# Projections begun inside the last head's step, and idle waits of TensorE filled with products that nobody reads

## The reference

```python
# first block: three branches of width 1024 each, one gated projection per branch
y_sb = stick_breaking_attention(sb_q, sb_k, sb_v)            # 8 heads of 128
y_s5 = s5_layer(s5_u, ..., s5_w_glu[l])                      # y * sigmoid(y @ w_glu)
y_ml = mlstm_chunkwise(ml_q_c, ml_k_c, ml_v, ...)            # 4 heads of 256
merged = jax.nn.sigmoid(g_sb) * (y_sb @ p_sb[l]) \
    + jax.nn.sigmoid(g_s5) * (y_s5 @ p_s5[l]) \
    + jax.nn.sigmoid(g_ml) * (y_ml @ p_ml[l])
x = x + gate1[:, None, :] * (merged @ w_out[l])
h = modulate(rms_norm(x, norm_moe_g[l]), shift2, scale2)
x = x + gate2[:, None, :] * hierarchical_moe(h, ...)         # 32 experts, top 2
x = rms_norm(x, final_g)
# second block: the same form with rglru (y_a), nsa (y_b, 8 heads), fox (y_c, 8 heads)
merged = (mg[:, :, 0] * (y_a @ w_branch[l, 0])
          + mg[:, :, 1] * (y_b @ w_branch[l, 1])
          + mg[:, :, 2] * (y_c @ w_branch[l, 2]))
h = h + merged @ w_out[l]
h = h + jax.nn.sigmoid(h @ w_ple_gate[l]) * e
```

## Time and profile before

| | |
|---|---|
| median of 3 runs | 3511.61 us (3509.37 to 3517.85) |
| the profiled execution | 3514.14 us, its span 3512.3 us |
| TensorE busy | 3034.3 us (86%) |
| POOL busy | 1687.8 us (48%) |
| DVE busy, ACT busy | 1183.7 us (34%), 1226.0 us (35%) |
| DMA, mean | 201 GB/s |

### The profile page before, as it was taken

The page is one execution under the profiler, slowest core; times in us unless marked ns, Lnnn a source line. Parts: engine busy times, 40 slices in busy tenths (PEclk is TensorE's granted clock), DMA queues, the critical chain, the costliest instruction groups (busy, mean ns, idle before and its releaser), DMA issues.

```text
span 3512.3 us, 52529 instructions
## 1 busy us (share of the span) xinstructions
PE 3034.3 (86%) x20592; PEld 2492.2 (71%) x20592; DVE 1183.7 (34%) x1660; ACT 1226.0 (35%) x1408; POOL 1687.8 (48%) x1296
## 2 busy tenths in 40 slices
PE   6999899898998987798889729778779988879898
PEld 1777588888898876443434229777779988869898
DVE  1488821134361323200000053265621124432335
ACT  1232332433544223211111124455534444444343
POOL 0000167676676764000000018745549976649897
PEclk8999989899999998899999959899989999989999
DMA  9432247375444865688899924432325543325443
GB/s 397 169 111 104 102 170 299 139 286 189 144 143 156 299 260 222 251 331 357 341 396 392 405 94 164 156 112 100 110 100 186 181 159 131 123 94 188 157 170 133
DMA packets 102014, 704.34 MB, mean 201 GB/s; under 512 B 11968, under 2 KB 15808, under 8 KB 17216
## 3 DMA queue, kind: packets, MB, share of 16 engines
q1 hardware_dynamic: 83088, 602.97, 45.9%
q10 hardware_dynamic: 15408, 74.86, 5.6%
q0 software_dynamic: 3392, 24.64, 1.7%
HBM read 723.92 MB, written 22.54 MB: 213 GB/s over the span
## 4 chain that ended last, share of the span: by engine, by line
PE 69%; DVE 11%; DMA 11%; ACT 6%; issue 3%; POOL 0%; DVEq 0%; ACTq 0%; SPq 0%; POOLq 0%
PE acc L549 58%; PE wk L549 10%; DMA ring<-in_moe 6%; DMA side_buf<-in_ada 2%; DMA stage<-in_ada 2%; ACT w_hi L1086 1%; ACT L1086 1%; DVE yl L1592 1%; DVE C_z L1595 1%; DVE rms_red L1604 1%; DVE C_sm L1592 0%; DVE A_t L1592 0%; DMA stage<-in_main 0%; ACT hb L1086 0%; ACT C_z L1086 0%
## 5 line engine op out<-in xcount | busy, mean ns | idle before, releaser
L525 POOL TENSOR_TENSOR w_lo<-stage,w_hi 128x512 fp32r<-128x512 f32 x1268 | 1672.8, 1351 | 1165.4 <-PE acc L549 720.4
L549 PE MATMUL acc<-xh,w_hi 128*128 128x256 f32 x3568 | 910.7, 294 | 29.0 <-DVE xl L1592 21.4
L549 PE MATMUL acc<-xl,w_hi 128*128 128x256 f32 x3568 | 897.8, 290 | 0.0
L549 PEld LDWEIGHTS acc<-xh,w_hi 128*128 128x128 f32 x3568 | 711.6, 199 | 72.6 <-issue 56.4
L549 PEld LDWEIGHTS acc<-xl,w_hi 128*128 128x128 f32 x3568 | 711.6, 199 | 0.7
L1086 ACT ACTIVATE w_hi<-stage 128x2048 fp32r<-128x2048 f32 x317 | 604.0, 1907 | 38.8 <-DMA stage<-in_main 38.7
L549 PE MATMUL acc<-xh,w_lo 128*128 128x256 f32 x3568 | 476.7, 287 | 0.4 <-POOL w_lo L525 0.4
L549 PEld LDWEIGHTS acc<-xh,w_lo 128*128 128x128 f32 x3568 | 451.9, 195 | 3.9 <-issue 2.3
L549 PE MATMUL acc<-ring,xg 128*64 128x512 f32 x1248 | 296.1, 616 | 55.0 <-DMA ring<-in_moe 54.3
L537 POOL DMA_DIRECT2D y_rows<-X_ysb x20 | 10.9, 547 | 638.0 <-ACT X_ysb L1086 638.0
L549 PEld LDWEIGHTS acc<-ring,xg 128*64 128x64 f32 x1248 | 96.9, 142 | 240.0 <-issue 239.1
(11 more groups left out here) (439 smaller groups left out, 3338.8 us busy)
## 6 DMA issues: line engine op xcount, KB each, us to landing
stage<-in_main SPq DMA_DIRECT2D x317, 1024.0 KB, 4.8
ring<-in_moe SPq DMA_DIRECT2D x234, 1024.0 KB
side_buf<-in_ada ACTq DMA_DIRECT2D x64, 1024.0 KB, 5.0
stage<-in_ada SPq DMA_DIRECT2D x32, 1024.0 KB, 8.1
stage<-in_sb SPq DMA_DIRECT2D x32, 1024.0 KB, 4.8
y_rows<-X_ysb POOLq DMA_DIRECT2D x19, 1024.0 KB, 10.2
x<-in_x ACTq DMA_DIRECT2D x1, 2048.0 KB, 12.7
out<-x SPq DMA_DIRECT2D x4, 512.0 KB, 5.4
```

What stands on the lines that cost most here:

```text
L525: last = pool.tensor_tensor(w_lo[:, k % 2, cs], stage[:, k, cs], w_hi[:, k, cs].bitcast(F32), ALU.subtract)
L549: return pe.matmul(o, w, r, start=start, stop=stop)
```

## The change

There are two parts.

**Opening and closing.** In the last step of each of the four head phases, where there was only the small work, `opening(name, i, tiles)` now does part of the output projection's chunks i = 0 to 3: for both output tiles all products with `w_hi` on the input tiles that are finished (7 of 8; in stage_b 6 of 8), and for i = 0 and 1 also those with `w_lo`. In the places where a step with a further head ran the small work in the middle of a chunk, it now runs between the two output tiles of the opening (`mid`). Behind the last step, `closing` adds what is left: the last tile (the last two in stage_b), and for i = 2 and 3 all 16 products with `w_lo`. Chunks 4 to 7 are as before. What is computed is the same.

**Spin products.** `spin(times, n)` multiplies `ones` by `ident`, 128x128 by 128 columns in plain float32, into columns of a PSUM bank that are free and that the next real product overwrites. It stands ahead of ten waits outside loops (glu 30, p_s5 24, wout 36, the channel sum and the router chunk behind wout 30 and 20, the combination of the experts 90, two channel sums 48 and 90, the first kv chunk 30, wout2 40 times) and, as `spin_in`, at the head of each step with a further head in stage_b (10, in 3 steps), stage_c (12, in 7 steps) and stage_d (5, in 7 steps).

```diff
+        def spin(times, n):
+
+            pe.wait_ge(evac_done, n - 3)
+            k = n % 4 if isinstance(n, int) else None
+            for _ in range(times):
+                mm(acc[:, k, T:T + P], ones[:], ident[:])
...
-        def beside(n, g, s, work):
+        def beside(n, g, s, work, name=None, i=0):
 
             if g is not None:
                 wide(*slot(n, g), mid=work if s is not None else None)
             else:
-                work()
+                opening(name, i, 7, mid=work)
...
+        def opening(name, i, tiles, h=yh, l=yl, mid=None):
+
+
+            k, q = slot(BASE[name] + i)
+            n = BASE[name] + i
+            pe.wait_ge(hi_ready, n + 1)
+            if n >= 4:
+                pe.wait_ge(evac_done, n - 3)
+            for c in range(2):
+                o = acc[:, k, c * T:(c + 1) * T]
+                for t in range(tiles):
+                    w = w_hi[:, k, (c * WT + t) * P:(c * WT + t + 1) * P]
+                    gm(o, w, h[:, t, :], c + t == 0)
+                    gm(o, w, l[:, t, :])
+                if mid and c == 0:
+                    mid()
+            if i < 2:
+                pe.wait_ge(lo_ready, n + 1)
+                for c in range(2):
+                    for t in range(tiles):
+                        gm(acc[:, k, c * T:(c + 1) * T], w_lo[:, k % 2, (c * WT + t) * P:(c * WT + t + 1) * P], h[:, t, :])
+
+        def closing(name, i, tiles, h=yh, l=yl):
+
+            k, q = slot(BASE[name] + i)
+            n = BASE[name] + i
+            for c in range(2):
+                for t in range(tiles, WT):
+                    w = w_hi[:, k, (c * WT + t) * P:(c * WT + t + 1) * P]
+                    gm(acc[:, k, c * T:(c + 1) * T], w, h[:, t, :])
+                    gm(acc[:, k, c * T:(c + 1) * T], w, l[:, t, :])
+            if i >= 2:
+                pe.wait_ge(lo_ready, n + 1)
+            for c in range(2):
+                for t in range(tiles if i < 2 else 0, WT):
+                    last = gm(acc[:, k, c * T:(c + 1) * T], w_lo[:, k % 2, (c * WT + t) * P:(c * WT + t + 1) * P], h[:, t, :],
+                              stop=t == WT - 1)
+            last.then_inc(chunk_done, 1)
...
             if g is not None:
                 plain(0, g)
+            else:
+                pe.wait_ge(yh_ready, 7)
+                opening("p_sb", 0, 7)
...
         pe.wait_ge(yh_ready, 8)
-        for t in range(8):
+        for i in range(4):
+            closing("p_sb", i, 7)
+        for t in range(4, 8):
             half(*slot(BASE["p_sb"] + t))
         pe.wait_ge(y5_ready, 9)
         beside_ada("g_sb", 0, wide)
+        spin(30, BASE["glu"])
         pe.wait_ge(y_split, 1)
         each(pe, BASE["glu"], 4, half)
         ada_columns(2, side_row[0])
+        spin(24, BASE["p_s5"])
         pe.wait_ge(y_split, 2)
...
             if s is not None:
+                if g is not None:
+                    spin_in(10, base_b, g, 2)
                 pe.wait_ge(qk_ready, s * 4 + 4)
...
                     wide(*slot(base_b + j, g, 2))
+                elif j < 4:
+                    opening("p_ml", j, 6)
...
+        spin(36, BASE["wout"])
         pe.wait_ge(mg_split, 1)
...
+        spin(30, BASE["router"])
         channel_sum(2)
+        spin(20, BASE["router"])
...
         pe.wait_ge(dg_ready, 1)
+        spin(90, BASE["kv"])
         pe.wait_ge(yg_in, 64)
...
+        spin(48, BASE["kv"])
         channel_sum(3)
+        spin(90, BASE["kv"])
         channel_sum(4)
+        spin(30, BASE["kv"])
...
+                    spin_in(12, base_c, g)
                 pe.wait_ge(c_d, s * NC_D + 1)
...
+                    spin_in(5, base_d, g)
                 pe.wait_ge(d_d, s * ND_D + 2)
...
+        spin(40, BASE["wout2"])
         pe.wait_ge(mg_split, 2)
```

More of the change, by code:

```diff
@@ L572, in chunk, with spin_in @@
             last.then_inc(chunk_done, 1)
+        def spin(times, n):
[3 more added lines that the diff above has]
+                mm(acc[:, k, T:T + P], ones[:], ident[:])
+        def spin_in(times, base, g, per=1):
+            k, q = slot(base, g, per)
+            pe.wait_ge(evac_done, q * 4 + k - 3)
+            for _ in range(times):
+                mm(acc[:, k, T:T + P], ones[:], ident[:])
         def wide(k, q, t=None, mid=None, split=None):
             chunk(k, q, 1, DT, xh, xl, mid, split)
-        def beside(n, g, s, work):
+        def beside(n, g, s, work, name=None, i=0):
             if g is not None:
@@ L599, in beside_plain, with gm @@
             else:
-                work()
+                opening("p_sb", j, 7, mid=work)
         def half(k, q, t=None):
             chunk(k, q, 2, WT, yh, yl)
+        def gm(o, w, r, start=False, stop=False):
+            return pe.matmul(o, w, r, start=start, stop=stop, skip_group_check=True)
+        def opening(name, i, tiles, h=yh, l=yl, mid=None):
[32 more added lines that the diff above has]
+            last.then_inc(chunk_done, 1)
         def half2(k, q, t=None):
@@ L709, in stage_a @@
                 plain(2, g)
+            else:
+                opening("p_sb", 2, 7)
             if s is not None:
@@ L778, in _ @@
             stage_b(i, i - 1)
+        pe.wait_ge(by_ready, 3)
         stage_b(None, 3)
         pe.wait_ge(by_ready, 4)
-        each(pe, BASE["p_ml"], 8, half)
+        for i in range(4):
+            closing("p_ml", i, 6)
+        each(pe, BASE["p_ml"] + 4, 4, half)
         beside_ada("g_ml", 2, wide)
+        spin(36, BASE["wout"])
         pe.wait_ge(mg_split, 1)
@@ L987, in stage_c @@
                 wide(*slot(base_c, g))
+            else:
+                opening("p_a", 0, 7)
             if s is not None:
@@ L995, in stage_c @@
                 last.then_inc(c_p, 1)
-            beside(base_c + 1, g, s, gates)
-            beside(base_c + 2, g, s, probs)
-            beside(base_c + 3, g, s, values)
+            beside(base_c + 1, g, s, gates, "p_a", 1)
+            beside(base_c + 2, g, s, probs, "p_a", 2)
+            beside(base_c + 3, g, s, values, "p_a", 3)
         stage_c(0, None, 0)
@@ L1006, in _ @@
         pe.wait_ge(c_d, 8 * NC_D)
-        each(pe, BASE["p_a"], 8, half)
+        for i in range(4):
+            closing("p_a", i, 7)
+        each(pe, BASE["p_a"] + 4, 4, half)
         each(pe, BASE["g_a"], 16, wide)
@@ L1049, in stage_d @@
                 wide(*slot(base_d, g))
-            beside(base_d + 1, g, s, scores)
-            beside(base_d + 2, g, s, probs)
-            beside(base_d + 3, g, s, values)
+            else:
+                opening("p_c", 0, 7)
+            beside(base_d + 1, g, s, scores, "p_c", 1)
+            beside(base_d + 2, g, s, probs, "p_c", 2)
+            beside(base_d + 3, g, s, values, "p_c", 3)
         heads(pe, stage_d)
         pe.wait_ge(d_d, 8 * ND_D)
-        each(pe, BASE["p_c"], 8, half)
+        for i in range(4):
+            closing("p_c", i, 7)
+        each(pe, BASE["p_c"] + 4, 4, half)
         each(pe, BASE["g_c"], 16, wide)
+        spin(40, BASE["wout2"])
         pe.wait_ge(mg_split, 2)
```

## The result

Predicted 3461 us (3438 to 3492). Measured in turn with the kernel before, on the same chip: 3460.5 us (median, 3457.9 to 3461.3) against 3513.1 (3509.4 to 3517.9). The ratio is 0.9848, 95% interval 0.9831 to 0.9865, so 53 us less by the medians. The profiled execution has a span of 3459.5 us.

What follows compares the result with a forecast made beforehand. It took TensorE's work, its waits and the lower clock behind them as the bound, POOL close behind. Openings 29 plus spin products 22 make 51 off 3511.6, giving 3461 us, range 3438 to 3492.

Steps and rivals of the forecast that it cites:

- Openings, stages a, c, d: Last steps and projections of these stages: projection products moved into TensorE's idle time gain 6.9, 13.1 and 9.2 us.
- Opening, stage_b: Stage_b's last step: the openings delay the `B_stm` products and DVE's last chain by 6.1 us, leaving a gain of 3.9.
- Stage_d: Spin products in stage_d's seven steps gain 1.1 us each, 8 in all, by keeping the clock up.
- Stage_b, loop: Spin products in three steps of stage_b gain 1.4 us each, 4 in all.
- Stage_c: Spin products in stage_c's seven steps gain 0.6 us each, 4 in all, with 3.1 us of the wait left idle.
- Groups outside loops: The ten spin groups outside loops gain 6 us together, 2.0 of it at p_s5 and 0 at the combination.
- Price of a constant product: Each spin product takes 0.225 us, 0.45 at the lower clock, and no group outlasts its wait while the clock stays up.
- The rule against the change: The skill says transposes against the identity do not count as clock activity, so products with `ident` might not hold the clock.
- The first rival: Spin products do not hold the clock and cost 50 us, the openings give 29 back: 3533 us; chance 0.04.
- The rests are too long: The clock falls in the idle time left behind each spin group, the spins give under 5: 3480 us; chance 0.22.
- eaten by the last steps: Openings delay DVE's and ACT's chains, giving 10 instead of 29: 3480 us, or 3496 with spins at 5; chance 0.12.
- everything closes: Openings give 33 and spin products 40: 3439 us; chance 0.12.

Runs made afterwards that it cites:

- run 1: The changed kernel with every `spin` and `spin_in` line left out, so openings and closings alone: 3484.9 us, ratio 0.9917 to the kernel before.
- run 2: Constant products alone, with the last steps and projections as in the kernel before: 3491.2 us, ratio 0.9941 to that kernel.
- run 4: The changed kernel with 14 constant products ahead of the wait for B_qk in stage_b's last step: 3455.9 us, ratio 0.9837 to the kernel before.
- run 3: The changed kernel with ten more constant products ahead of the wait for C_zc in seven steps of stage_c: 3454.6 us, ratio 0.9827 to the kernel before.
- run 8: The changed kernel with 22 constant products ahead of C_qs, 10 ahead of C_zc, 24 and 8 in the last steps of stage_c and stage_d: 3451.2 us.
- run 11: The changed kernel without the twelve constant products at the head of stage_c's steps: 3458.9 us, ratio 0.9842 to the kernel before.
- run 6: The changed kernel without the ten `spin` groups outside loops, the three `spin_in` kept: 3461.4 us, ratio 0.9855 to the kernel before.
- run 5: The changed kernel with each constant product written as two transposes of the same tiles: 3463.0 us, ratio 0.9858 to the kernel before.
- run 9: The changed kernel with 14 constant products in stage_b's last step, 20, 10, 24 in stage_c, 8 in stage_d's last step, 116 ahead of the combination: 3434.1 us.
- run 10: The changed kernel with 15 constant products instead of 5 at the head of stage_d's seven steps: 3478.9 us, ratio 0.9896 to the kernel before.
- run 7: The changed kernel with stage_a's opening of chunk 0 moved behind the last head's next small product: 3456.9 us, ratio 0.9845 to the kernel before.

## Why the prediction was right, step by step

- **The sum** was right (51 against 53), and so was its split: 29 and 22 predicted, 29 and 23 in runs 1 and 2. But the 22 was right by compensation, which is luck: by the marks the places give 5.9, 0.4, 13 and 7.5 where 4, 4, 8 and 6 stood. These 26.8 and the openings' 29.7 make 56.5; the two executions differ by 52.8. Most of the rest is 2.6 us lost in g_sb (1.1 of waiting for `side_buf` and a dip behind it, which run 1's trace doesn't have) and 1.1 from wout to the second block.
- **Openings, stages a, c, d**: 6.9, 13.1, 9.2 predicted, 6.3, 13.0, 9.4 found. The working held in its parts: between the marks POOL's first low part behind the last step came 2.7, 9.5 and 5.8 us earlier (3, 9 and 5 foreseen), the last-head products wait less than they are held up, and POOL's low parts then set the pace. POOL was the bound longer than foreseen: six low parts follow one another (29.9 us), not three, so the gain is counted at the seventh chunk. TensorE's waits in the closings of these three stages were 4.0 and 0.3 to 0.8 us, not 4 and 2.5: the clock fell in each first one, and the products behind it ran at half speed through what would have been the second. In stage_a the working on POOL and DVE held as well (the last section has the numbers).
- **Opening, stage_b**: 3.9 predicted, 1.0 found; this step failed, and it failed for a reason outside it. The opening alone gives 3.6 (run 1). In the changed kernel the products behind the 4.0 us wait for B_qk ran at 1.2 GHz for 10 us, with the first opening among them, and the B_stm products started 8.1 us behind DVE's instruction for their operand (1069.56 less 1061.50), where it was 0.75 before (1076.20 in the earlier trace rows less 1075.45): 7.3 late, 6.1 foreseen. Fourteen constant products gave 4.5 back (run 4). The prediction had counted constant products per loop step and never asked what the last step, which has none, would inherit: run 2 shows it without any opening, 1.8 us lost there.
- **Stage_d**: 8 predicted, 13 found (the first product of the last head comes 42.9 us earlier and the start of stage_d 29.8). The prediction valued one dip a step at 1.1 of 1.7 us, in seven steps. In the trace five of the seven had two dips of 3.4 us each, one behind the wait for E_qks and one behind that for E_z (1.9 us, filled by nothing), and the first and second had none. With the first wait filled both went, and such a step fell from 34.1 to 31.1. Only one of the seven kept one (32.6). So the number of steps was too high and the worth of one too low.
- **Stage_b, loop**: 4 predicted, 5.9 found.
- **Stage_c**: 4 predicted, 0.4 found; this step failed. It said that the wait for C_zc had left the clock alone. It had done so only in the steps with a dip for C_qs; the first step, which has no wait for C_qs, had a dip behind its wait for C_zc already in the kernel before (2283.5 to 2286.9). In the changed kernel the partly filled wait for C_qs kept its dip in four of six steps, about as often as the prediction's 0.6 of 2.1 us says, and in the two others the C_zc wait of 2.9 us had its own (2471.71), so that these were only 0.4 us shorter than before. And the first step paid the full 2.7 us, where the prediction had said that no group outlasts its wait. Runs 3, 8 and 11 show the sizes: filling the first wait alone gives nothing, both with rests of 3.1 and 0.6 us give 9.2, both with under 1 us give 13.1, or 15.3 without the first step.
- **Groups outside loops**: 6 predicted, 7.5 by the marks, 9.9 by the trace of run 6 and 2.5 by its ratio, which can't tell them apart. By the starts of POOL's low parts p_s5 gave 2.1 (2.0 predicted), glu none (0.5), wout 0.9 and wout2 1.4 (0.8 and 0.4), and 3.1 came behind p_s5 in g_s5, which the prediction didn't have. One trace of a group is worth little, though: of the eleven traces with these groups seven still have a dip of 3.4 us behind the wait of wout, seven behind that of wout2 and three behind that of p_s5, and with it 1.3 to 1.6 us less gain. The combination gave none, as predicted: its rest was 8.2 us and the clock behind it 0.79. The channel sums and the first kv chunk (2 together) showed nothing.
- **Price of a constant product**: 0.225 us predicted. 587 of them, two records each, take 138.9 us, 0.237 in the mean with some at the lower level. That none outlasts its wait failed in the first steps of stage_c and stage_d, 3.8 us together.

```profile
L549 PE MATMUL acc<-ident,ones 128*128 128x128 f32 x1174 | 138.9, 279 | 0.0
```

- **The rule against the change** (the Trainium skill, "TensorE: Matmul & The Clock Gate", Part 4: a transpose does not count as activity). Nothing here bears it out: products with the identity held the clock, and so did real transposes (run 5, where each left one record and a product two). The first rival, at 0.04, was rightly low.
- **Rivals.** "The rests are too long" (0.22) was true for the combination and for four of six steps of stage_c only; "eaten by the last steps" (0.12) for stage_b only; "everything closes" (0.12) came within reach in run 9, by filling what the change had left.

## What to carry to other kernels

A dip of the clock belongs to a chain of waits, not to one: before filling a wait, list the next ones behind it (1.9 us was long enough for a dip in run 10), and look at the step's length and at the clock behind each of them, not at the idle time. Filling the first was enough in stage_d and gave nothing in stage_c. Look at each step of a loop apart: the first may lack the wait, and there the filling is pure cost. Filling a loop and leaving its last step bare moved the loss into that step here (stage_b). Work begun early on one engine pays until the next engine in line (here POOL, 5.05 us a chunk against 5.7) is the bound; count the gain at the chunk where that ends. A constant product too many costs its full price (0.225 us here), and can shift a later wait so that it dips as well (run 10 cost twice its surplus).

## What the runs showed of the hardware that was not expected

- Transposes against the identity kept TensorE's clock up as well as products: 0.99 over six steps of stage_d with either (run 5).
- The same wait of 1.9 us for E_z left the clock alone in most steps of 31.1 us and was followed by a dip in most steps once these were 1 us longer (runs of the changed kernel and run 10). In stage_c a dip behind one wait and none behind the next changed places from step to step (run 3). The length of a wait alone does not tell whether the clock falls.
- POOL's low part and DVE's work slowed each other where they met, as the prediction took from the earlier trace rows. POOL's first two chunks of p_sb took 11.9 to 12.1 us, and two of DVE's instructions beside them (`A_vr`, 128x256) 2.8 to 2.9, in the kernel before and in run 7; in the changed kernel, where DVE's rotation comes later, they took 10.06 and 0.85.
- Executions differ by some us where the code is the same: POOL's third low part of p_sb started at 459.9 to 464.4 us in the traces with the opening in its old place, and the last projection has two forms that are 4.8 us apart (run 6). A gain of under 5 us is better read between two marks of the trace than from the medians, and from more than one trace.
